# Stick-breaking attention with running sums of weights and neighbours' differences of values

## What is computed

```python
z = jnp.einsum('bhqd,bhkd->bhqk', qb, kb) * scale
mask = kpos < qpos
log_beta = jax.nn.log_sigmoid(z)
log_1m_beta = jnp.where(mask, jax.nn.log_sigmoid(-z), 0.0)
log_a = log_beta + lax.cumsum(log_1m_beta, axis=3, reverse=True) - log_1m_beta
a = jnp.where(mask, jnp.exp(log_a), 0.0)
outs.append(jnp.einsum('bhqk,bhkd->bhqd', a.astype(vb.dtype), vb))
```

## Time and profile before

| | before |
|---|---|
| median of 3 runs | 1923.89 us (1923.82 to 1924.07) |
| profiled execution | 1924.49 us, of which the span is 1922.5 us |
| PE busy | 1911.0 us, 99% |
| DVE busy | 1392.9 us, 72% |
| ACT busy | 786.7 us, 41% |
| POOL busy | 152.1 us, 8% |
| values | about 784 to 833 us of the span |
| pooling branch | about 833 to 871 us |
| attention with gates | about 871 to 1153 us |
| DMA packets | 246,723, of which 16,368 are under 512 B |

### The profile page before, as it was taken

The page is one execution under the profiler, slowest core; times in us unless marked ns, Lnnn a source line. Parts: engine busy times, 40 slices in busy tenths (PEclk is TensorE's granted clock), DMA queues, the critical chain, the costliest instruction groups (busy, mean ns, idle before and its releaser), DMA issues.

```text
span 1922.5 us, 25204 instructions
## 1 busy us (share of the span) xinstructions
PE 1911.0 (99%) x9046; PEld 1599.3 (83%) x9046; DVE 1392.9 (72%) x1714; ACT 786.7 (41%) x1170; POOL 152.1 (8%) x221
## 2 busy tenths in 40 slices
PE   9999999999999999999999999999999999999998
PEld 9888888888888888888888888898888888888886
DVE  6977867774566776786878878879777777755655
ACT  7423232323434543345665652464323232334344
POOL 1000000000000300002443420010000000000002
PEclk9999999999999999999999999999999999999999
DMA  5456654558676534248446347643545444677665
GB/s 165 147 198 228 225 174 149 189 196 312 210 236 196 185 110 151 73 134 236 142 127 175 105 154 254 191 136 114 182 141 197 148 168 153 220 265 240 204 195 200
DMA packets 246723, 347.19 MB, mean 181 GB/s; under 512 B 16368, under 2 KB 150256, under 8 KB 243056
## 3 DMA queue, kind: packets, MB, share of 16 engines
q1 hardware_dynamic: 246640, 346.10, 55.3%
HBM read 232.79 MB, written 112.98 MB: 180 GB/s over the span
## 4 chain that ended last, share of the span: by engine, by line
PE 95%; DVE 2%; DMA 1%; ACT 1%; issue 1%; POOL 1%; SPq 0%; POOLq 0%; DVEq 0%; ACTq 0%
PE bank L1233 39%; PE bank L1330 10%; PE bank L1277 8%; PE bank L1278 8%; PE bank L1279 8%; PE bank L1187 5%; PE bank L1471 4%; PE bank L1379 2%; PE bank L1407 2%; PE bank L1437 2%; PE bank L1543 2%; PE bank L1162 1%; PE bank L1562 1%; PE bank L1561 1%; PE bank L1528 1%; PE bank L1526 1%
## 5 line engine op out<-in xcount | busy, mean ns | idle before, releaser
L2171 DVE TENSOR_TENSOR dn_lo<-dn_lo_raw,dn_hi 128x1024 fp32r<-128x1024 f32 x149 | 181.9, 1223 | 150.9 <-ACT dn_hi L1741 150.5
L1233 PE MATMUL bank<-lo_t,wa_hi 128*128 128x512 f32 x640 | 249.0, 389 | 0.0
L1233 PE MATMUL bank<-hi_t,wa_hi 128*128 128x512 f32 x640 | 249.0, 389 | 0.0
L1233 PE MATMUL bank<-hi_t,wa_lo 128*128 128x512 f32 x640 | 249.0, 389 | 0.0
L1741 ACT ACTIVATE dn_hi<-dn_lo_raw 128x1024 fp32r<-128x1024 f32 x149 | 157.9, 1060 | 219.3 <-DMA dn_lo_raw<-act_dram 219.3
L1277 PE MATMUL bank<-dn_hi 128*128 128x512 f32 x596 | 232.5, 390 | 0.0
L1279 PE MATMUL bank<-dn_lo,dn_hi 128*128 128x512 f32 x596 | 231.9, 389 | 0.0
L1278 PE MATMUL bank<-dn_hi,dn_lo 128*128 128x512 f32 x596 | 231.9, 389 | 0.0
L1233 PE MATMUL bank<-hi_b,wa_hi 128*128 128x512 f32 x480 | 186.9, 389 | 0.9 <-DVE up L2295 0.9
L1233 PE MATMUL bank<-lo_b,wa_hi 128*128 128x512 f32 x480 | 186.8, 389 | 0.0
L1233 PE MATMUL bank<-hi_b,wa_lo 128*128 128x512 f32 x480 | 186.7, 389 | 0.0
(11 more groups left out here) (275 smaller groups left out, 3764.1 us busy)
## 6 DMA issues: line engine op xcount, KB each, us to landing
wa_lo_raw<-in_ffn_w_gate_up_dram SPq DMA_DIRECT2D x87, 512.0 KB, 4.9
dn_lo_raw<-act_dram SPq DMA_DIRECT2D x149, 256.0 KB, 4.3
act_dram<-g SPq DMA_DIRECT2D x44, 512.0 KB, 4.3
wd_t<-in_ffn_w_down_dram SPq DMA_DIRECT2D x44, 512.0 KB, 6.6
act_dram<-s_of SPq DMA_DIRECT2D x88, 256.0 KB, 6.4
wd_dram<-wd_t SPq DMA_DIRECT2D x22, 1024.0 KB, 5.9
dn_lo_raw<-wd_dram SPq DMA_DIRECT2D x85, 256.0 KB, 3.4
dn_lo_raw<-in_ffn_w_down_dram SPq DMA_DIRECT2D x64, 256.0 KB, 3.1
```

The costliest lines, as they stand in the source:

```text
L1233: last = nc.tensor.matmul(acc, lhs, rhs, start=n == 0 and i != 2 and i < 5, stop=n == 11, skip_group_check=True)
L2171: return nc.vector.tensor_tensor(dst, raw, hi.bitcast(f32), ALU.subtract)
```

## The change

A key's weight is A[s] = beta[s] * product of the later keeps. The sum C[s] of the weights from key s to the last satisfies C[s] = keep[s] * C[s+1] + beta[s], since keep = 1 - beta; where beta is 0 at the masked end, C stays 0 whatever keep is. So one scan with the sigmoids as second operand makes C in place, the multiply is left out, and only `a` is masked. The output is the sum of A[s] v[s], which is the sum of C[s] (v[s] - v[s-1]) with v[-1] = 0, so the values in `v_w` become differences of neighbours:

- `take_v` is one copy on DVE of all 512 columns of a tile out of PSUM; ACT has none. All four pairs are stored, as raw rows, to `v_dram`, which has a row of zeros ahead of token 0.
- For each pair four loads bring the rows and the rows one earlier, for each of two heads, in runs of 64 numbers. The loads of the first two pairs stand on SP's queue between unit 3's pooling weights and `spill_pool_branch(1)`, those of the others at steps 20 and 36.
- At steps 0, 6, 26 and 42 DVE subtracts (`differences`), ACT rounds (`differences_hi`), and a step later DVE makes the low parts (`differences_lo`). PE's `weigh` waits for these.

```diff
+V_STEPS = (0, 6, 2 * NT + 10, 4 * NT + 10)
...
-        tail_p = at("tail_p", [P, SEQ], f32, o + 16384)
...
-        v_dram = nc.dram_tensor("v_dram", (2, P, 2 * SEQ), f32, kind="Internal").ap()
+        v_dram = nc.dram_tensor("v_dram", (1 + SEQ, BR, P), f32, kind="Internal").ap()
...
+            sp_.wait_ge(const_set, 3)
+            sp_.dma_start(v_dram[0].rearrange("s p -> p s"), zero_col[:, :].to_broadcast([P, BR]),
+                          allow_slow_non_contiguous=True).then_inc(v_in[0], 16)
             store_h(0, range(4, NT))
...
-                sp_.dma_start(v_dram.rearrange("s p n -> p s n")[:, :, t * 2 * P:(t + 1) * 2 * P],
-                              value_place(t).rearrange("p s e a c -> p s (e a c)").bitcast(f32)).then_inc(v_sp[t % 4], 16)
+                sp_.dma_start(v_dram[1 + t * P:1 + (t + 1) * P].rearrange("p s n -> p (s n)"),
+                              value_place(t)).then_inc(v_sp[t % 4], 16)
...
+            def load_v(k):
+
+                if k >= 2:
+                    sp_.wait_ge(pv_ok, NT * (k - 1))
+                elif k == 0:
+                    for i in range(4):
+                        sp_.wait_ge(v_sp[i], 32)
+                    for i in range(3):
+                        sp_.wait_ge(ring_sp[i], 32 * ring_uses(i))
+                    sp_.wait_ge(ylo, 4)
+                    sp_.wait_ge(v_in[0], 16)
+                for a, row in ((0, 1), (1, 0)):
+                    for e in range(2):
+                        sp_.dma_start(v_raw[:, k % 2, :, e, a, :],
+                                      v_dram[row:row + SEQ, PAIR_ORDER[k], e * HD:(e + 1) * HD].rearrange("(t p) c -> p t c", p=P)
+                                      ).then_inc(v_in[k % 2], 16)
...
             pool_branch_unit(3)
+            load_v(0)
+            load_v(1)
             spill_pool_branch(1)
...
-                for pair in range(2):
-                    if s == NT * (2 + 2 * pair) + 4:
-                        load_v(pair)
+                for k in (2, 3):
+                    if s == 2 * NT * (k - 1) + 4:
+                        load_v(k)
...
-                if x_["pair"] < 2 and pn % NT == 0:
-                    pe.wait_ge(v_in[slot], 16)
+                if pn % NT == 0:
+                    pe.wait_ge(v_split, 3 * (pn // NT) + 3)
...
-                    act.wait_ge(scan_ok, n - 1)
+                    act.wait_ge(a_ok, n - 1)
...
+            def differences_hi(k):
+
+                act.wait_ge(v_split, 3 * k + 1)
+                nc.scalar.activation(v_w[:, k % 2, :, :, 0, :], v_raw[:, k % 2, :, :, 1, :], ACT.Copy).then_inc(v_split, 1)
...
-                hi_taken()
-                acc = bank[:, (t + 4) % 8, :].rearrange("p (m s e c) -> p m s e c", m=2, s=2, e=2)
-                nc.vector.tensor_tensor(v_w[:, :, t, :, 1, :], acc[:, 1], v_w[:, :, t, :, 0, :].bitcast(f32), ALU.subtract)
-                nc.vector.tensor_tensor(value_place(t)[:, :, :, 1, :], acc[:, 0], value_place(t)[:, :, :, 0, :].bitcast(f32),
-                                        ALU.subtract).then_inc(acc_free[t % 4], 1)
+                dve.wait_ge(acc_ready, V_READY[t])
+                if t > 4:
+                    dve.wait_ge(v_sp[t % 4], 16)
+                nc.vector.tensor_copy(value_place(t), bank[:, (t + 4) % 8, :]).then_inc(acc_free[t % 4], 1)
...
-                dve.wait_ge(masked, 2 * n + 2)
-                if n:
-                    dve.wait_ge(a_ok, n)
-                nc.vector.tensor_tensor_scan(tail_p[:, 0:w][:, ::-1], keep[:, n % 2, 0:w][:, ::-1],
-                                             zero_col[:, :].to_broadcast([P, w]), 1.0, ALU.mult, ALU.add).then_inc(scan_ok, 1)
-                dve.wait_ge(scan_ok, n + 1)
-                b = weights_of(n)[:, 0:w - 1]
-                nc.vector.tensor_tensor(b, b, tail_p[:, 1:w], ALU.mult).then_inc(a_ok, 1)
+                dve.wait_ge(masked, n + 1)
+                row = weights_of(n)[:, 0:w][:, ::-1]
+                nc.vector.tensor_tensor_scan(row, keep[:, n % 2, 0:w][:, ::-1], row, 0.0, ALU.mult, ALU.add).then_inc(a_ok, 1)
+
+            def differences(k):
+
+                slot = k % 2
+                dve.wait_ge(v_in[slot], 64 * (k // 2 + 1) + (0 if slot else 16))
+                now, before = (v_raw[:, slot, :, :, a, :] for a in range(2))
+                nc.vector.tensor_tensor(before, now, before, ALU.subtract).then_inc(v_split, 1)
+
+            def differences_lo(k):
+
+                slot = k % 2
+                dve.wait_ge(v_split, 3 * k + 2)
+                nc.vector.tensor_tensor(v_w[:, slot, :, :, 1, :], v_raw[:, slot, :, :, 1, :],
+                                        v_w[:, slot, :, :, 0, :].bitcast(f32), ALU.subtract).then_inc(v_split, 1)
...
-                for dst, fill in ((keep[:, n % 2, w - P:w], 1.0), (weights_of(n)[:, w - P:w], 0.0)):
-                    nc.gpsimd.affine_select(out=dst, in_=dst, compare_op=ALU.is_gt, fill=fill, base=0,
-                                            pattern=[[-1, P]], channel_multiplier=1).then_inc(masked, 1)
+                last = weights_of(n)[:, w - P:w]
+                nc.gpsimd.affine_select(out=last, in_=last, compare_op=ALU.is_gt, fill=0.0, base=0,
+                                        pattern=[[-1, P]], channel_multiplier=1).then_inc(masked, 1)
```

More of the change, by code:

```diff
@@ L339, in macaron_layer @@
         sg2 = at("sg2", [P, 2, HALF], f32, base + 108 * K)
-        v_w = at("v_w", [P, 2, NT, 2, 2, HD], f32r, X0)
+        v_w, v_raw = both("v_w", [P, 2, NT, 2, 2, HD], X0)
         ring_raw = [at(f"ring_raw{i}", [P, SEQ], f32, X0 + 8192 * RING_AT[i]) for i in range(3)]
@@ L381, in macaron_layer @@
         pst = at("pst", [P, 4, HALF], f32, base + 144 * K)
-        v_st = at("v_st", [P, 4, 2, 2, 2, HD], f32r, base + 144 * K)
-        v_first = at("v_first", [P, 2, 2, 2, HD], f32r, X0 + 40960)
+        v_st = at("v_st", [P, 4, BR * P], f32, base + 144 * K)
+        v_first = at("v_first", [P, BR * P], f32, X0 + 40960)
         yt_lo, yt_raw = both("yt_lo", [P, 4, BR // 2, HALF], base + 112 * K)
@@ L515, in macaron_layer @@
         masked = sem("masked")
-        scan_ok = sem("scan_ok")
+        v_split = sem("v_split")
         a_ok = sem("a_ok")
@@ L652, in value_place @@
         def value_place(t):
-            return v_st[:, t % 4] if t else v_first[:, :]
+            return v_st[:, t % 4, :] if t else v_first[:, :]
         def pool_place(u, b):
@@ L1006, in load_head @@
                         sp_.dma_start(q_st[half, slot, c0:c1].bitcast(f32), qk_dram[part, pair, rows, c0:c1]).then_inc(quarter_in if hn == 0 and c0 == 0 else landed, 16)
[L1008 to L1013, removed]
             load_head(0)
@@ L1936, in values_hi @@
                 nc.scalar.activation(w_hi[:, par], w_raw[:, par], ACT.Copy).then_inc(whi, 1)
[L1938 to L1950, removed]
             def pool_hi(m, ab):
@@ L2030, in _ @@
             pool_hi(0, 1)
-            take_v(0)
-            take_v(1)
             take_group(0)
             pool_hi(1, 0)
-            take_v(2)
-            take_v(3)
             pool_hi(1, 1)
@@ L2040, in _ @@
             sums_of_y_hi(0, 1)
[L2041 to L2044, removed]
+            for slot, sums in ((2, 3), (3, 3), (1, 4)):
+                sums_of_y_hi(slot, sums)
             first_pool_part(0)
@@ L2128, in _ @@
                     betas(s)
+                if s in V_STEPS:
+                    differences_hi(V_STEPS.index(s))
                 if s == NA + DRAIN - 1:
@@ L2905, in _ @@
                     split_piece(j, piece)
+                if s in V_STEPS:
+                    differences(V_STEPS.index(s))
+                if s - 1 in V_STEPS:
+                    differences_lo(V_STEPS.index(s - 1))
             def outputs_sum(i):
```

## The result

| | before | after |
|---|---|---|
| median of 18 runs each | 1924.64 us (1923.55 to 1925.26) | 1928.26 us (1926.75 to 1929.44) |
| profiled execution, its span | 1924.49 us, 1922.5 us | 1927.19 us, 1925.3 us |

The ratio is 1.0020, 95% interval 1.0013 to 1.0026: 3.6 us slower, about 0.2%. The forecast was 1924.1 us, 0.2 us over the median it started from.

A forecast was written before the change was run, and what follows sets the result against it. TensorE, busy 99% of the span, was taken as the bound. Attention -1.9 us plus a pooling-branch stall of +2.1, all else 0, gave +0.2 us on the 1923.9 us median: 1924.1 us, range 1921.7 to 1930.9.

The forecast's parts named there:

- No change that can be told: Whole kernel: the time stays within about 0.2%, 3.8 us, of the kernel before; chance 0.76.
- The gain of 1.9 us: Attention: with DVE's multiply gone, four TensorE stalls ahead of transposes go; -1.9 us, bounds -2.3 and 0.
- The scan at its old price: Attention, DVE: the scan with sigmoids as second operand costs what the old one did, 2290 ns for 1024 elements.
- The loads and the order of the queue: Pooling branch: eight early loads, 1.15 us each, delay unit 1's stores on SP's queue; TensorE waits +2.1 us in unit 2.
- The rival of dear loads: Early loads: at two packet slots per short packet, 2.3 us a load, TensorE waits 11.3 us, time 1933.3; chance 0.20.
- The rival of hidden loads: Early loads: at 0.9 us each, or if stores don't queue behind them, nothing stalls; -1.9, or 1922.0 us; chance 0.22.
- Price 0 for the keys and gate weights behind the loads: After the early loads: engines catch up, some 6 us free of 9.2 added, so transfers queued behind add no stall.
- The later loads: Attention: two later groups, 4.6 us each, have 16 steps of lead while the engines are about half busy; price 0.
- price 0 for the new waits at steps 6, 26 and 42: Attention: ACT's wait for DVE's subtraction and DVE's for ACT are covered by the removed multiplies; 0, bounds 0 and +3 us.
- the case stood among the rivals at 0.06: Attention: the new waits at steps 6, 26 and 42 hold ACT, one tile late each time; +3, 1927.1 us; chance 0.06.

## Why the prediction was near and where it failed

The time is inside the range. No change that can be told (within 0.2%), the likeliest case, holds barely: 0.19%, interval 0.13 to 0.26%. The point is 3.4 us off the difference (+0.2 forecast, +3.6 measured). That the time is in the range is in part luck: the range's upper part stood there for dear loads, which did not come, and a term priced at 0 used it. By its own steps:

- **The gain of 1.9 us** was right in place and size: the four stalls vanished, and the multiply alone, left out, gave 1.9 us in the trace (-2.5 in the medians). What made these four tiles late was not only the length of the chain; see the last section.
- **The scan at its old price** was right: 2291 ns for 1024 elements, and 88 us in all where 92 were named.
- **The loads and the order of the queue** were right in mechanism. 17,136 packets under 512 bytes were added (17,000 forecast). The loads took 9.8 us for 9.2, block 3's store landed at 860.68 for 860.1, and the stall was 2.9 us for 2.1. A load took 1.2 us, 19 ns a packet and engine, and 1.1 to 1.2 us over the five kernels where these loads follow unit 3's weights, for the 1.15 forecast. Moving one pair took the stall away; moving both behind the stores moved it to the next unit.
- **The rival of dear loads**, two packet slots for a short run, fell. The Trainium skill ("DMA: Bandwidth & Descriptors", Specifications) has full rate only from 512 bytes and a read-modify-write below. The runs agree that 256 bytes stay under the rate of 512 (224 against 299 GB/s) and show no doubling: 2 MB took 9.8 or 9.1 us in runs of 256 bytes and 8.1 in runs of 512. Whether anything was read and written again, no run shows.
- **The rival of hidden loads** had its price too low: 32 packets of 31 ns are 1.0 us a load, not 0.9, so the store would land at 858.8 and leave a stall of 0.8 us, not 0.1. Loads at about that price were run (8.1 us for eight times 256 KB), and 1.6 us of stall stayed.
- **Price 0 for the keys and gate weights behind the loads** was nearly right: 0.4 us on the weight loads of two operands, 0.3 us more stall than before between 871 and 892 us. The later loads had 6 steps and not 16 until DVE wanted them (at steps 26 and 42); it did not wait for them.
- **The step that failed: price 0 for the new waits at steps 6, 26 and 42.** The prediction said they were covered by the multiplies that DVE no longer makes. It cost 2.5 us, near its own bound of +3, and the case stood among the rivals at 0.06. DVE's room is the wrong cover: DVE could have made the subtraction earlier (at step 26 it was idle for 1.4 us until 987.0), but on its program it stands behind a turned low part and, at step 26, a piece of gate weights, so it is late by order and not by load. The engine that pays is ACT, held 2.07 and 1.47 us, with three instructions, 2.0 us from start to start, between the end of the wait and the next turned copy. Step 6 indeed cost nothing: there the subtraction began at 905.03, ACT's sigmoids ended at 905.31, ACT waited 0.97 us, and only 1.4 us lay between the end of the wait and the next turned copy; PE had no stall. With the same subtraction and no wait of ACT the cost is gone.

## What to carry to other kernels

A wait that ties two engines inside one step is priced on the engine that waits, by what is queued behind it and how soon a third engine needs that; spare time on the engine that is waited for is no cover when its program puts the awaited instruction late. Give such a pair a step of slack each way. Transfers put ahead of stores on one queue delay whatever buffer those stores set free: count who writes that buffer next, in this unit and the one after, before choosing their place.

## What was not expected of the hardware

After 4.8 us from the start of one matmul to that of the next, in the kernel with the loads behind the stores, its granted clock was 0.51 for some 3 us, so that a stall of 4.6 us cost 6.2; after the pause of 3.1 us in the kernel after no such drop shows (1.00 from 861.4 on).

DVE and POOL hold each other up. In the kernel without the paired wait a DVE subtraction of 1024 elements took 2.31 us where POOL multiplied beside it from 987.03 to 988.44, against 1.21 to 1.24 us at the other three steps. In the kernel after a scan of 768 elements took 2.57 us at 899.69, beside a POOL product from 899.35 to 900.65, and 1.75 us at 932.35. It goes the other way too: each of the 16 selects that POOL started during a scan in the kernel after ended 0.09 us behind that scan and took 1.1 to 1.8 us, where beside DVE's low parts, which read PSUM, a select took 0.29 us. A scan of 640 elements in the kernel before (1.49 us where no product ran) beside a product, and a scan and a select in the kernel after:

```profile
932.51 1.72 POOL L3041 TENSOR_TENSOR gst<-gst,pool_y 128x512 f32<-128x512 f32 x1
933.01 2.57 DVE L2866 TENSOR_TENSOR_SCAN tail_p<-keep,zero_col 128x640 f32<-128x640 f32 x1
...
932.35 1.75 DVE L2867 TENSOR_TENSOR_SCAN a<-keep,a 128x768 f32<-128x768 f32 x1
932.54 1.65 POOL L3048 TENSOR_SCALAR_AFFINE_SELECT a<-a 128x128 f32<-128x128 f32 x1 [1.83 <-ACT a L2077]
```

In the kernel before five of the 64 scans took 0.8 to 1.1 us longer than others of their width, each beside a product of POOL (896.45, 933.01, 1007.23, 1063.88, 1096.92), and four of the five stand just ahead of the four stalls of the earlier trace rows. In the kernel after only two scans are held. So these stalls came where a product of POOL held the chain of scan and multiply. Leaving the multiply out made room enough: without it a scan at 931.48 still took 2.58 us, and no stall followed. Whether moving POOL's products alone would give back the 1.9 us was not tested.
